# A hybrid decoder layer in split fp32r: from the pooling gates on, the tokens become the stationary operand and 512 weight columns the moving one

## The chip, the core and the metric

The kernel runs on one core of one Trainium2 chip, as one launch. The metric is the device time of that core in microseconds (us); before the change it is 2078.82 us, the median of three runs. The engines are named as in the profile: PE is TensorE's matmuls and PEld its loads of the stationary operand, ACT is ScalarE, DVE is VectorE, POOL is GpSimd, and SP is the sync engine, whose queue issues the weight transfers.

## The reference

One layer over 256 tokens of 2048 features, batch 1, all float32. Cut to what matters:

```
h      = rmsnorm(x, g_pre_mix)
proj   = h @ w_in                # -> z, xbc, dt, u_pool, gate_ssm, gate_pool
y_ssm  = mamba2_branch(...)      # 4096 features;   y_pool = pooling branch, 2048 features
merged = sigmoid(gate_ssm) * (y_ssm @ w_ssm_out) + sigmoid(gate_pool) * (y_pool @ w_pool_out)
x      = x + rmsnorm(merged @ w_mix_out, g_post_mix)
g, u   = split(rmsnorm(x, g_pre_ffn) @ w_ffn_in)          # 5632 features each
x      = x + rmsnorm((silu(g) * u) @ w_ffn_out, g_post_ffn)
x      = x + sigmoid(x @ w_ple_gate) * (p @ w_ple_proj)
```

## The kernel before

**Layout.** Everything between the first and the last transposition is features x tokens: a tile holds 128 features on the partitions and the 256 tokens in the free dimension. So a product takes a 128x128 block of weights as the stationary operand, streams the 256 tokens of one 128-feature block of the input through it, and leaves 128 output features x 256 tokens in PSUM.

**Precision.** A float32 operand is split in two fp32r parts, hi and lo, and a product is three matmuls: hi x hi, lo x hi and hi x lo. For the weights ACT makes the hi part (`w_hi`, a copy; `hi_units`), DVE the lo part (`w_lo`, a subtraction; `lo_units`). The same is done once for each operand built on the chip (`h_hi`/`h_lo`, `m_hi`/`m_lo`, `act_hi`/`act_lo`, `p_hi`/`p_lo`).

**The stream of weights.** All weights come in *units*: two 128-row blocks of 512 columns, 512 KB. `w_raw`, `w_hi` and `w_lo` are rings of four. SP issues unit u when DVE has finished unit u-4, ACT splits unit u when PE has used unit u-4, DVE follows ACT, PE follows DVE. A unit costs PE 2 blocks x 4 groups of 128 columns x 3 = 24 matmuls of 256 moving columns:

```
for n in columns:
    o = accum[:, n, :]
    wh = w_hi[:, s, a, P * n:P * n + P]
    wl = w_lo[:, s, a, P * n:P * n + P]
    mm(o, wh, hi[:, b, :], b == 0 and n % 2 == 0, False)
    mm(o, wh, lo[:, b, :], False, False)
    last = mm(o, wl, hi[:, b, :], False, b == blocks - 1)
```

**Order.** The stages run in a fixed order written out for each engine: the B/C projections, eight SSD groups, the pooling branch; then those that the change touches, 492 units in all: PO (pooling gate and `w_pool_out`, 64 units), SO (SSM gate and `w_ssm_out`, 96), MIX (`w_mix_out`, 32), FF (`w_ffn_in`, 11 chunks of 16 = 176), FO (`w_ffn_out`, 88), PP (`w_ple_proj`, 4), PG (`w_ple_gate`, 32). A product accumulates in `acc[0]` or `acc[1]` (two PSUM banks each), and ACT or DVE take it out while the next one runs (`acc_taken`). Work between units is hung in by `after=` hooks: what stands at hook k of an engine comes in its own order right after its unit k.

**Norms.** ACT squares the accumulated chunk, DVE adds three of the four chunks, and PE sums over the partitions with a float32 matmul against `mean_w`, which leaves the mean at every partition (`three_quarters`, `last_quarter`, `x1_squares`, four matmuls each). Then ACT takes the root, DVE the reciprocal of 256 columns, and `residual` multiplies and adds. The last chunk of MIX and of PG is done in two halves, so that what follows can begin on the first.

**Output.** `rows_out` turns 128x128 blocks of the result on PE, ACT or DVE copies them to `o_rows`, SP sends them out. The transposed x goes to DRAM at the start (`xT_scratch`) and comes back before FF (`x_back`).

## Time and profile before

| | |
|---|---|
| median of three runs | 2078.82 us (2078.63 to 2080.57) |
| span of the profiled execution, first to last instruction | 2083.3 us |
| mean granted TensorE clock in it | 0.994 |
| PE busy, PEld busy | 99%, 98% |
| DVE busy, ACT busy | 59%, 48% |
| moved by DMA | 384.55 MB, mean 185 GB/s |

Of the profiled execution only the span is known; it is 4.5 us above the median of the plain runs. Busy time of PE is a union over pipelined instructions (one matmul record lasts 0.28 us while the next starts some 0.12 us later), so the pace of the matmuls is read from counts over stretches, not from the duration of one.

### The profile page before, as it was taken

The numbers are of one execution on the slowest core, as the hardware profiler recorded it, in microseconds if no ns is written. First come the engines' busy times: TensorE is split into PE (matmuls) and PEld (weight loads), VectorE is DVE, ScalarE is ACT, GpSimd is POOL, SyncE is SP. The second block draws the span as 40 slices with busy tenths as digits, with TensorE's granted clock in tenths as the row PEclk, the third lists the DMA queues.
The fourth block names the chain that finished last, engine by engine and source line by source line (L and its number), as shares of the span: only waits on it lengthen the run. The fifth ranks groups of instructions, "written<-read, shape, count | busy, mean of one in ns | idle before, by whom it ended". The sixth has DMA issues, their size and how long they took to land.

```text
span 2083.3 us, 42373 instructions
## 1 busy us (share of the span) xinstructions
PE 2056.3 (99%) x17268; PEld 2042.0 (98%) x17268; DVE 1238.2 (59%) x1293; ACT 1002.5 (48%) x1149; POOL 2.4 (0%) x40
## 2 busy tenths in 40 slices
PE   7999999999999999999999989999999999999999
PEld 6999999999999999999999989999999999999998
DVE  5877888888776444444444475555555554444474
ACT  4545666666646444344444464444444443444453
POOL 0000000000000000000000000000000000000000
PEclk8999999999999999999999999999999999999999
DMA  6666666666565666555555646666666665555454
GB/s 207 203 203 192 188 190 191 186 186 188 171 191 189 186 182 183 188 184 183 184 187 183 218 131 184 187 184 182 184 187 182 183 188 185 183 186 187 158 189 140
DMA packets 199813, 384.55 MB, mean 185 GB/s; under 512 B 12176, under 2 KB 19504, under 8 KB 198448
## 3 DMA queue, kind: packets, MB, share of 16 engines
q1 hardware_dynamic: 199504, 381.16, 59.2%
q10 hardware_dynamic: 224, 2.16, 0.3%
q8 instruction: 65, 1.06, 0.2%
q14 instruction: 20, 0.16, 0.0%
HBM read 379.01 MB, written 4.26 MB: 184 GB/s over the span
## 4 chain that ended last, share of the span: by engine, by line
PE 98%; DVE 1%; ACT 1%; SPq 0%; issue 0%; DMA 0%; ACTq 0%
PE acc L397 94%; PE bank L397 2%; PE pair L397 1%; PE bank L400 0%; DMA dsk_row<-in_d_skip_dram 0%; PE pair L400 0%; ACT w_hi L661 0%; SPq L290 0%; ACT L661 0%; DVE csum L1258 0%; DVE w_lo L1037 0%; PE acc L400 0%; SPq L286 0%; DVE yrstd L1222 0%; DVE rstd L1048 0%
## 5 line engine op out<-in xcount | busy, mean ns | idle before, releaser
L1037 DVE TENSOR_TENSOR w_lo<-w_raw,w_hi 128x1024 fp32r<-128x1024 f32 (+1 forms) x696 | 847.7, 1221 | 801.9 <-ACT w_hi L661 801.8
L661 ACT ACTIVATE w_hi<-w_raw 128x1024 fp32r<-128x1024 f32 (+1 forms) x696 | 732.6, 1057 | 953.7 <-PE acc L397 946.7
L397 PE MATMUL acc<-h_hi,w_hi 128*128 128x256 f32 x3712 | 1052.6, 284 | 12.7 <-DVE h_lo L1044 6.3
L397 PE MATMUL acc<-h_lo,w_hi 128*128 128x256 f32 x3712 | 1044.4, 281 | 0.0
L397 PE MATMUL acc<-h_hi,w_lo 128*128 128x256 f32 x3712 | 1044.3, 281 | 0.0
L397 PEld LDWEIGHTS acc<-h_hi,w_hi 128*128 128x128 f32 x3712 | 702.4, 189 | 15.9 <-issue 8.2
L397 PEld LDWEIGHTS acc<-h_lo,w_hi 128*128 128x128 f32 x3712 | 702.4, 189 | 2.2 <-issue 1.9
L397 PEld LDWEIGHTS acc<-h_hi,w_lo 128*128 128x128 f32 x3712 | 702.2, 189 | 0.0
L397 PE MATMUL acc<-act_hi,w_hi 128*128 128x256 f32 x704 | 198.1, 281 | 0.0
L397 PE MATMUL acc<-act_lo,w_hi 128*128 128x256 f32 x704 | 197.9, 281 | 0.0
L397 PE MATMUL acc<-act_hi,w_lo 128*128 128x256 f32 x704 | 197.9, 281 | 0.0
L397 PE MATMUL acc<-y_lo,w_hi 128*128 128x256 f32 x512 | 144.0, 281 | 0.0
L397 PE MATMUL acc<-y_hi,w_lo 128*128 128x256 f32 x512 | 144.0, 281 | 0.0
L397 PE MATMUL acc<-y_hi,w_hi 128*128 128x256 f32 x512 | 143.9, 281 | 0.0
L397 PEld LDWEIGHTS acc<-act_hi,w_hi 128*128 128x128 f32 x704 | 132.9, 189 | 0.0
L397 PEld LDWEIGHTS acc<-act_lo,w_hi 128*128 128x128 f32 x704 | 132.9, 189 | 0.0
L397 PEld LDWEIGHTS acc<-act_hi,w_lo 128*128 128x128 f32 x704 | 132.9, 189 | 0.0
L397 PEld LDWEIGHTS acc<-y_hi,w_hi 128*128 128x128 f32 x512 | 96.7, 189 | 0.0
L397 PEld LDWEIGHTS acc<-y_lo,w_hi 128*128 128x128 f32 x512 | 96.7, 189 | 0.0
L397 PEld LDWEIGHTS acc<-y_hi,w_lo 128*128 128x128 f32 x512 | 96.7, 189 | 0.0
L397 PE MATMUL acc<-m_hi,w_hi 128*128 128x256 f32 x256 | 72.2, 282 | 0.0
L397 PE MATMUL acc<-m_hi,w_lo 128*128 128x256 f32 x256 | 72.0, 281 | 0.0
(186 smaller groups left out, 1613.9 us busy)
## 6 DMA issues: line engine op xcount, KB each, us to landing
w_raw<-in_w_in_dram SPq DMA_DIRECT2D x256, 512.0 KB, 3.8
w_raw<-in_w_ffn_in_dram SPq DMA_DIRECT2D x176, 512.0 KB, 3.7
w_raw<-in_w_ffn_out_dram SPq DMA_DIRECT2D x88, 512.0 KB, 3.6
w_raw<-in_w_ssm_out_dram SPq DMA_DIRECT2D x64, 512.0 KB, 3.6
w_raw<-in_w_pool_out_dram SPq DMA_DIRECT2D x32, 512.0 KB, 3.7
w_raw<-in_w_mix_out_dram SPq DMA_DIRECT2D x32, 512.0 KB, 3.6
w_raw<-in_w_ple_gate_dram SPq DMA_DIRECT2D x32, 512.0 KB, 3.6
decay<-cum_scratch SPq DMA_DIRECT2D x8, 1024.0 KB, 6.1
```

What stands on the lines that cost most here:

```text
L397: return nc.tensor.matmul(o, lhsT=l, rhs=r, start=first, stop=last, skip_group_check=True)
L661: return nc.scalar.activation(o, i, fn, **kw)
L1037: v.tensor_tensor(low, raw, high.bitcast(F32), ALU.subtract).then_inc(w_lo_done, 1)
```

## The change

From PO on, `row_product` takes the place of `product`. A 128-token block of the input is now stationary, and the 512 columns of a weight block stream past it; the result is 128 tokens x 512 features, one PSUM bank for each half of the tokens. A unit is 2 blocks x 2 halves x 3 = 12 matmuls of 512 moving columns. `acc_rows` are the same banks as `acc`.

The next product needs its input as features x tokens again, so the merged chunks (`turn_merged`), the FFN's activations (`turn_act`), the x after the mixers (`turn_x1`) and the x after the FFN (`turn_x2`) are turned on PE in 128x128 blocks, into `pair` or into four half-bank `pieces`. Norms are now along the free dimension: ACT squares with a running sum per token (`row_squares`), DVE adds four numbers, root and reciprocal are on one column. The gains of the post-norms come as rows broadcast to all partitions (`gain_mix`, `gain_ff`). x is read again as it lies in DRAM, so the trip of the transposed x is gone, and so are the matmuls against `mean_w` behind the first norm, `rows_out`, and the copies to `o_rows`: the output leaves as it is computed. The loads of x, the gain and p move from SP's queue to ACT's, at hook 3 of MIX's first chunk.

```diff
-            sp.wait_ge(unit_used, 4 * Q_MIX)
-            sp.wait_ge(xT_stored, 16)
-            sp.dma_start(x_back[:, :, :], xT_dram).then_inc(xT_landed, 16)
-            sp.dma_start(p_in[:, :, :], p_rows).then_inc(p_landed, 16)
...
+            for j in range(NQ - 1):
+                sp.wait_ge(o_ready, j + 1)
+                sp.dma_start(out_rows[:, :, CW * j:CW * j + CW], o_tok[:, j]).then_inc(out_stored, 16)
+            for a in range(2):
+                sp.wait_ge(o_ready, NQ + a)
+                sp.dma_start(out_rows[:, a, D - CW:D], o_tok[:, NQ - 1, a]).then_inc(out_stored, 16)
...
+            def row_products(q, k0, k, blocks, hi, lo, rows, halves):
+                s = (k0 + k) % RING
+                for i in range(2):
+                    b = 2 * k + i
+                    wh, wl = w_hi[:, s, i, :], w_lo[:, s, i, :]
+                    for a in halves:
+                        t = slice(P * a, P * a + P)
+                        mm(rows[:, a, :], hi[:, b, t], wh, b == 0, False)
+                        mm(rows[:, a, :], hi[:, b, t], wl, False, False)
+                        last = mm(rows[:, a, :], lo[:, b, t], wh, False, b == blocks - 1)
+                return last
+            def row_product(c, q, k0, blocks, hi, lo, rows, wait_for=None, after=None, halves=False):
+                pe.wait_ge(acc_taken, c - 1)
+                units = blocks // 2
+                for k in range(units):
+                    if wait_for:
+                        wait_for(k)
+                    if not halves or k < units - RING:
+                        pe.wait_ge(w_lo_done, 4 * q + k0 + k + 1)
+                    elif k == units - RING:
+                        for late in range(k, units):
+                            pe.wait_ge(w_lo_done, 4 * q + k0 + late + 1)
+                            last = row_products(q, k0, late, blocks, hi, lo, rows, (0,))
+                        last.then_inc(half_done, 1)
+                    own = (1,) if halves and k >= units - RING else (0, 1)
+                    row_products(q, k0, k, blocks, hi, lo, rows, own).then_inc(unit_used, 1)
+                    if after:
+                        after(k)
+            def turn_chunk(src):
+                for n in range(NB):
+                    for a in range(2):
+                        last = turn(pair[:, n, P * a:P * a + P], src[:, a, P * n:P * n + P])
+                return last
+            def turn_piece(halves, k, turned):
+                for n in range(2):
+                    for a in range(2):
+                        c = P * (2 * k + n)
+                        last = turn(pieces[k % 4][:, n, P * a:P * a + P], halves[a][:, c:c + P])
+                last.then_inc(turned, 1)
...
-                product(C_PO + 2 * j, Q_PO + 4 * j, 0, KB, h_hi, h_lo, acc[0])
-                product(C_PO + 1 + 2 * j, Q_PO + 4 * j, 8, KB, yp_hi, yp_lo, acc[1],
-                        wait_for=lambda k: k % 2 == 0 and yp_quarter(k))
+                row_product(C_PO + 2 * j, Q_PO + 4 * j, 0, KB, h_hi, h_lo, acc_rows[0])
+                row_product(C_PO + 1 + 2 * j, Q_PO + 4 * j, 8, KB, yp_hi, yp_lo, acc_rows[1],
+                            wait_for=lambda k: k % 2 == 0 and yp_quarter(k))
+            def turn_merged(j):
+                pe.wait_ge(fam["op_m"][0], j + 1)
+                if not (isinstance(j, int) and j == 0):
+                    pe.wait_ge(fam["op_m"][2], j)
+                turn_chunk(prod).then_inc(m_turned, 1)
+            def so(j, first):
+                row_product(C_SO + 2 * j, Q_SO + 6 * j, 0, KB, h_hi, h_lo, acc_rows[0],
+                            after=lambda k: k == 3 and not first and turn_merged(j - 1))
+                row_product(C_SO + 1 + 2 * j, Q_SO + 6 * j, 8, 2 * KB, y_hi, y_lo, acc_rows[1])
...
-                product(C_MIX + j, Q_MIX + 2 * j, 0, KB, m_hi, m_lo, acc[j % 2],
-                        wait_for=lambda k: j == 0 and k % 2 == 0 and pe.wait_ge(fam["op_m"][2], k // 2 + 1),
-                        after=lambda k: j == NQ - 1 and k == 5 and three_quarters(RMS_MIX, sqs1),
-                        halves=j == NQ - 1)
-            for half, ready, count in ((0, sq_half, 1), (1, sq_ready, NQ * RMS_MIX + NQ)):
-                pe.wait_ge(ready, count)
-                for n in (2 * half, 2 * half + 1):
-                    last = mm(ss, mean_w[:, :], sq1[:, (NQ - 1) % 2, n, :], False, n == NB - 1)
-            last.then_inc(sq_used, 1)
...
+                row_product(C_MIX + j, Q_MIX + 2 * j, 0, KB, m_hi, m_lo, acc_rows[j % 2],
+                            wait_for=lambda k: j == 0 and k % 2 == 0 and pe.wait_ge(fam["op_m"][2], k // 2 + 1),
+                            after=lambda k: j == 0 and k == 3 and turn_merged(NQ - 1), halves=j == NQ - 1)
+            def turn_x1(k):
+                pe.wait_ge(x1_ready, (2, 3, 4, 4, 5, 5, 6, 6)[k])
+                if k >= 4:
+                    pe.wait_ge(fam["op_h"][2], PIECES + k - 3)
+                turn_piece((x1[:, 1, :], x1[:, 0, :]), k, x1_turned)
...
+            row_product(C_FF, Q_FF, 0, KB, h_hi, h_lo, acc_rows[0], after=x1_ahead,
+                        wait_for=lambda k: pe.wait_ge(fam["op_h"][2], PIECES + k + 1))
...
+            def turn_act(j):
+                pe.wait_ge(acc_taken, C_FF + 2 * j + 2)
+                if isinstance(j, int) and j == 0:
+                    pe.wait_ge(fam["op_p"][2], 1)
+                else:
+                    pe.wait_ge(fam["op_ff"][2], j)
+                turn_chunk(uff).then_inc(ff_turned, 1)
...
+            def ff(j):
+                row_product(C_FF + 2 * j, Q_FF + 4 * j, 0, KB, h_hi, h_lo, acc_rows[0],
+                            after=lambda k: k == 4 and turn_act(j - 1))
+                row_product(C_FF + 1 + 2 * j, Q_FF + 4 * j, 8, KB, h_hi, h_lo, acc_rows[1])
...
+            def turn_x2(k):
+                pe.wait_ge(x2_ready, (2, 4, 6, 6, 8, 8, 10, 10)[k])
+                if k >= 4:
+                    pe.wait_ge(fam["op_x2"][2], k - 3)
+                turn_piece((fg[:, 0, :], fg[:, 1, :]), k, x2_turned)
...
-            def rows_out(j):
-                pe.wait_ge(o_ready, j + 1)
-                if not (isinstance(j, int) and j == 0):
-                    pe.wait_ge(rows_ready, j)
-                for a in range(2):
-                    for n in range(NB):
-                        last = turn(pair[:, 2 * a:2 * a + 2, :].rearrange("p b t -> p (b t)")[:, P * n:P * n + P],
-                                    o_T[:, n, P * a:P * a + P])
-                last.then_inc(ot_done, 1)
...
+                if c == NQ - 1:
+                    for k in range(4):
+                        turn_x2(k)
+                row_product(C_PP + c, Q_PP, c, 2, p_hi, p_lo, acc_rows[c % 2])
...
+                row_product(C_PG + j, Q_PG + 2 * j, 0, KB, h_hi, h_lo, acc_rows[j % 2],
+                            wait_for=lambda k: j == 0 and pe.wait_ge(fam["op_x2"][2], k + 1),
+                            after=lambda k: j == 0 and k + 4 < PIECES and turn_x2(k + 4), halves=j == NQ - 1)
...
+            def merged_hi(j):
+                act.wait_ge(m_turned, j + 1)
+                f(m_hi[:, ds(4 * j, 4), :], pair[:, :, :]).then_inc(fam["op_m"][1], 1)
...
+                        act.wait_ge(unit_used, 4 * Q_MIX)
+                        act.dma_start(x_rows_in[:, :, :], x_rows).then_inc(tok_landed, 16)
+                        act.dma_start(gain_mix[:, :], g_post_mix.to_broadcast([P, D])).then_inc(tok_landed, 16)
+                        act.dma_start(p_in[:, :, :], p_rows).then_inc(tok_landed, 16)
...
+            act.wait_ge(half_done, 1)
+            row_squares(RMS_MIX, NQ - 1, 0, acc_rows[1])
+            act.wait_ge(row_sum, 1)
+            row_root(RMS_MIX, slice(0, 1), 4 * EPS)
+            hi_units(Q_FF, 0, 2)
+            act.wait_ge(unit_used, 4 * Q_FF)
+            row_squares(RMS_MIX, NQ - 1, 1, acc_rows[1])
+            act.wait_ge(row_sum, 2)
+            row_root(RMS_MIX, slice(1, 2), 4 * EPS)
+            hi_units(Q_FF, 2, 2)
...
+                    last = f(h_hi[:, b, :], pieces[k % 4][:, n, :], scale=vecs[:, V_PRE_FFN + b:V_PRE_FFN + b + 1])
+                last.then_inc(fam["op_h"][1], 1)
...
+                if lag and k == 7:
+                    act.wait_ge(ff_turned, j)
+                    f(act_hi[:, ds(4 * (j - 1), 4), :], pair[:, :, :]).then_inc(fam["op_ff"][1], 1)
...
+            def post_gain(j, gain, rows):
+                cols = slice(CW * j, CW * j + CW)
+                by_feature = gain[:, cols].unsqueeze(1).to_broadcast([P, 2, CW])
+                v.tensor_tensor(fg[:, :, cols], rows, by_feature, ALU.mult).then_inc(acc_taken, 1)
...
+                v.scalar_tensor_tensor(x1[:, 1 - a, c0:c1], fg[:, a, c0:c1], rows_std[:, RMS_MIX, a:a + 1],
+                                       x_rows_in[:, a, c0:c1], ALU.mult, ALU.add).then_inc(x1_ready, 1)
...
+            last_gain(0)
+            row_inverse(RMS_MIX, 0)
+            dve.wait_ge(row_rstd, 1)
+            x1_part(0, 0, D)
+            lo_units(Q_FF, 0, 2)
+            dve.wait_ge(row_sq, 2 * NQ)
+            row_sums(RMS_MIX, 1)
+            last_gain(1).then_inc(acc_taken, 1)
+            row_inverse(RMS_MIX, 1)
+            dve.wait_ge(row_rstd, 2)
+            dve.wait_ge(acc_taken, C_FF)
+            x1_part(1, 0, 2 * P)
+            x1_part(1, 2 * P, 4 * P)
+            lo_units(Q_FF, 2, 1)
+            x1_part(1, 4 * P, 8 * P)
             for k in range(PIECES):
-                if k + 1 == PIECES - 2:
...
+                x1_low(k)
                 if k:
                     lo_units(Q_FF, k + 2, 1)
+                if k < 2:
+                    x1_part(1, (8 + 4 * k) * P, (12 + 4 * k) * P)
...
+                        dve.wait_ge(ff_turned, j - 1)
+                    for a in range(2):
+                        last = v.scalar_tensor_tensor(uff[:, a, :], acc_rows[1][:, a, :], rows_aux[:, 1, a:a + 1],
+                                                      graw[:, a, :], ALU.mult, ALU.mult)
+                    last.then_inc(acc_taken, 1)
...
+                    lo_part("op_ff", j, act_lo[:, four, :], pair[:, :, :], act_hi[:, four, :])
...
+                    v.scalar_tensor_tensor(fg[:, a, c0:c1], fg[:, a, c0:c1], rows_std[:, RMS_F, a:a + 1],
+                                           x1[:, 1 - a, c0:c1], ALU.mult, ALU.add).then_inc(x2_ready, 1)
...
+            dve.wait_ge(row_sq, 4 * NQ + 2)
+            v.tensor_reduce(rows_std[:, RMS_F, :], ssq[:, RMS_F, :, :], axis=AX.X, op=ALU.add).then_inc(row_sum, 1)
+            post_gain(NQ - 1, gain_ff, acc_rows[1])
+            dve.wait_ge(row_std, 4)
+            both = rows_std[:, RMS_F, :]
+            v.reciprocal(both, both).then_inc(row_rstd, 1)
+            dve.wait_ge(row_rstd, 6)
+            dve.wait_ge(acc_taken, C_PP)
+            x2_part(0, 2 * P)
+            x2_part(2 * P, 4 * P)
+            x2_part(4 * P, 8 * P)
+            lo_units(Q_PP, 3, 1)
...
+                lo_part("op_x2", k + 1, h_lo[:, 2 * k:2 * k + 2, :], pieces[k % 4], h_hi[:, 2 * k:2 * k + 2, :])
+                lo_units(Q_PG, k, 1)
+                if k < 2:
+                    x2_part((8 + 4 * k) * P, (12 + 4 * k) * P)
```

## Rows read from the trace of the kernel before

**Rows 1.** The page, part 1: busy us (share of the span) and instructions.

```profile
PE 2056.3 (99%) x17268; PEld 2042.0 (98%) x17268; DVE 1238.2 (59%) x1293; ACT 1002.5 (48%) x1149; POOL 2.4 (0%) x40
```

**Rows 2.** The page, part 4: the chain that ended last, by engine.

```profile
PE 98%; DVE 1%; ACT 1%; SPq 0%; issue 0%; DMA 0%; ACTq 0%
```

**Rows 3.** Groups by shape: busy us, mean ns of one, idle before and its releaser.

```profile
L1037 DVE TENSOR_TENSOR w_lo<-w_raw,w_hi 128x1024 fp32r<-128x1024 f32 x692 | 844.9, 1224 | 796.5 <-ACT w_hi L661 796.3
...
L661 ACT ACTIVATE w_hi<-w_raw 128x1024 fp32r<-128x1024 f32 x692 | 730.1, 1059 | 948.0 <-PE acc L397 941.0 <-DMA w_raw<-in_w_in_dram 6.0 <-PE bank L397 0.5
...
L397 PEld LDWEIGHTS acc<-h_hi,w_hi 128*128 128x128 f32 x3712 | 702.4, 189 | 15.9 <-issue 8.2 <-DVE h_lo L1044 6.7 <-DVE w_lo L1037 0.6
```

**Rows 4.** The chain in order of time, whole span: start us, us, what.

```profile
577.93 615.45 PE acc L397 x5184
1193.38 1.73 PE bank L397 x8
...
1216.38 1.73 PE bank L397 x8
...
1237.97 692.06 PE acc L397 x5832
1930.03 1.73 PE bank L397 x8
```

**Rows 5.** Four stretches: us, each engine busy (instructions), granted clock, DMA share, GB/s.

```profile
680.00:1180.00 500.00, 500.00 (x4216) 500.00 (x4215) 234.08 (x193) 210.69 (x210) 0.00 (x0) 1.00 0.58 185
1250.00:1900.00 650.00, 650.00 (x5480) 650.00 (x5479) 341.45 (x284) 266.85 (x260) 0.00 (x0) 1.00 0.61 184
1206.50:1209.50 3.00, 3.00 (x15) 3.00 (x15) 3.00 (x4) 2.46 (x5) 0.00 (x0) 0.50 0.00 0
1197.79:1205.95 8.16, 1.98 (x11) 1.28 (x9) 6.38 (x8) 6.27 (x11) 0.00 (x0) 0.81 0.43 127
```

**Rows 6.** The same chain from 1925 us on, five pieces of it.

```profile
1968.82 1.03 ACT sq_f L661
...
1969.90 2.00 PE bank L397 x8
...
2065.05 0.87 PE pair L400 x8
...
2079.33 0.67 PE pair L400 x4
...
2080.03 0.69 DVE o_rows L1443
```

**Rows 7.** Groups by shape, DVE.

```profile
L1186 DVE TENSOR_TENSOR decay<-decay,cbm 128x2048 f32<-128x2048 f32 x8 | 18.3, 2284 | 0.0
...
L1225 DVE SCALAR_TENSOR_TENSOR yg<-yg,vecs,yrstd 128x256 f32<-128x256 f32 x32 | 13.4, 480 | 1.0
...
L1438 DVE SCALAR_TENSOR_TENSOR o_T<-tgate,ple 128x512 f32<-128x512 f32 x2 | 1.4, 692 | 9.0 <-ACT tgate L661 9.0
...
L1180 DVE TENSOR_TENSOR to_end<-decay,tok_cum 128x8 f32<-128x8 f32 x8 | 1.3, 158 | 0.0
```

**Rows 8.** Groups by shape, ACT: busy us, mean ns of one, idle before.

```profile
L661 ACT ACT_TABLE_LOAD x25 | 32.1, 1283 | 1.2 <-PEq L1458 0.8
...
L661 ACT ACTIVATE sq<-acc 128x512 f32<-128x512 f32 x2 | 1.2, 598 | 4.9 <-PE acc L397 4.9
```

**Rows 9.** DMA from 1175 to 1215 us: rate by slice; issues with KB, us to landing.

```profile
GB/s 336 39 219 272 287 303 410 410 442 315 369 401 399 393 395 297 68 16 0 0 63 219 289 201 254 119 313 104 10 0 0 0 0 0 0 113 375 53 0 104
...
w_raw<-in_w_ffn_in_dram SPq DMA_DIRECT2D x9, 512.0 KB, 5.0
x_back<-xT_scratch SPq DMA_DIRECT2D x1, 2048.0 KB, 9.6
```

More of the change, by code:

```diff
@@ L649, in _ @@
-            for half in range(2):
-                pe.wait_ge(o_ready, NQ + half)
-                pe.wait_ge(rows_ready, NQ - 1)
-                for a in range(2):
-                    for n in range(2):
-                        last = turn(pair[:, 2 * half + a, P * n:P * n + P], o_T[:, 2 * half + n, P * a:P * a + P])
-                last.then_inc(ot_done, 1)
+                    row_product(C_FO + j, Q_FO + t * (FO_UNITS // 2), FO_UNITS * i, FF // P, act_hi, act_lo,
+                                acc_rows[i],
+                                wait_for=lambda k: j == 0 and k % 2 == 0 and pe.wait_ge(fam["op_ff"][2], k // 2 + 1),
+                                after=lambda k: j == 0 and k == 4 and turn_act(NFF - 1))
@@ L879, in _, with post_squares @@
                 so(j, Q_SO + 6 * j, False)
-            def post_take(stage, j, q, k_end, accum, first, squares, gain, between=None):
+            def post_squares(stage, j, q, k_end, rows):
                 summed(q, k_end)
-                if j == NQ - 1:
-                    act.wait_ge(sq_added, SQ_ADDED[stage] + 1)
-                f(squares[:, j % 2] if j else first, accum[:, :, :], ACT.Square).then_inc(sq_ready, 1)
-                if between:
-                    between()
-                for n in range(NB):
-                    col = gain + NB * j + n
-                    last = f(fg[:, NB * j + n, :], accum[:, n, :], scale=vecs[:, col:col + 1])
-                last.then_inc(acc_taken, 1)
+                for a in range(2):
+                    row_squares(stage, j, a, rows)
             for j in range(NQ):
```

420 lines of the change are left out of this document (184 added, 236 removed).

## The prediction, made blind

> **What bounds the kernel now.** The page's first part comes first: PE and its weight loads are busy through 99% and 98% of the span, DVE 59%, ACT 48% [rows 1]. A union of pipelined records says only that PE is hardly ever without work, so the chain that ended last is next: 98% of it is PE [rows 2]. The groups by shape confirm it from the other side: nearly all idle time of ACT before its weight splits ends with PE, and DVE's ends with ACT [rows 3]. Nothing waits long for a transfer. So what counts is how many nanoseconds PE needs from one matmul to the next, and the counts give that: 615.45 us for 5184 and 692.06 us for 5832 matmuls in a row, 118.7 ns each [rows 4], which agrees with 500 us for 4216 and 650 us for 5480 [rows 5].
>
> Where do the 118.7 ns go? In 1206.5:1209.5 the granted clock is at its lower level, 1.2 GHz, and 15 records touch 3.00 us, 14 spacings of 214 ns: 256 columns at one per cycle are 213.3 ns, so next to nothing comes on top [rows 5]. At 2.4 GHz, the clock of the long stretches, 256 columns are 106.7 ns, so here 12.0 ns are on top of each. The float32 matmuls against `mean_w` are the third point: eight records of 256 columns in 1.73 us, 216.3 ns each at full clock [rows 4]; eight turns of 128 columns take 0.87 us, 109 ns each [rows 6]. The 128 further columns cost 107.5 ns, two cycles each, so such a record streams for 213.3 ns with 3.0 ns on top, although each has a fresh 128x128 stationary block too. The surcharge is thus about 12 ns where streaming lasts 107 ns in fp32r and 0 to 3 ns where it lasts 213 ns. I read it as a load of the next block that just fails to hide behind 107 ns of streaming. The change doubles the streaming per load.
>
> **The products.** From PO on there are 492 units of two blocks, 984 blocks. Before, a block is 4 x 3 = 12 matmuls, 11,808 in all: x 118.7 ns = 1401.6 us. After, it is 2 x 3 = 6 of 512 columns, 5,904 in all. Columns in total stay the same. The trace has no fp32r matmul of 512 columns, so I bound it. From below: 512 columns at 2.4 GHz with nothing on top, 213.3 ns, 1259.3 us. From above: the whole surcharge stays, 213.3 + 12.0 = 225.3 ns, 1330.2 us; further above, the cost goes with the columns, 2 x 118.7 = 237.4 ns, and nothing is gained. The nearest row is the `mean_w` record, which streams just as long: 216.3 ns [rows 4], 1277.0 us. I take that: **-124.6 us**.
>
> The Trainium skill (TensorE: Matmul & The Clock Gate, "Back-to-back issue gap") gives N/2.4 + 2.5 ns between warm matmuls. For 512 columns that is an estimated 215.8 ns, near the row; for 256 columns it is 109.2 ns, where this trace has 118.7. By the rule alone a split into two costs 2.5 ns, 15 us over all, and the change would have no more to win; but the kernel before is timed by its trace, and behind the change the rule ends at the forecast's own time.
>
> **The turns.** Added while PE streams: merged 4 x 8, activations 11 x 8, x1 4 pieces x 4 (the first four pieces fall into a gap, below), x2 8 x 4: 168 turns x 109 ns [rows 6] = **+18.3 us**; p is turned before and after. Removed: three `rows_out` of eight, **-2.6 us**. None should make PE wait. `turn_act` stands after PE's unit 4, some 13 us into a chunk of 2.6 us units; its input is ready after a split of ACT (1.06), of DVE (1.22, [rows 3]) and two operations of 0.69 us on 512 columns [rows 7], under 5 us. Behind it on ACT are the copy out of `pair` and the split of unit 8, on DVE the lo part and its own: some 5 us after unit 4, while PE reaches unit 8 after 8.7. For `turn_merged`, after unit 3, DVE has its two operations behind its unit 4, ready by about 8 us of 10.4. If this cover were gone, each of the 15 groups would cost its wait whole.
>
> **The norms.** In the stream of before stand the three quarters of MIX, four groups for x1, the three quarters of F: 6 x 1.73 = 10.4 us [rows 4]; at the end of FO PE waits 1.1 us for a square (1.03), then sums for 2.0 [rows 6]. All of it goes: **-13.5 us**.
>
> **MIX to FF.** Before, PE's last product of MIX ends at 1197.79 and the first of FF starts at 1205.95, 8.16 us, with a few sums between [rows 5]. After, the first half of the tokens is ready 4 x 6 x 0.216 = 5.2 us before the end. ACT squares it (0.60, [rows 8]), loads a table (1.28) and takes the root; DVE goes on with gain (0.69), a residual of 2048 columns (2.28), two splits (2.44) and is free 2.5 us after the end. Then, in its queue: sum 0.16, gain 0.69, reciprocal 0.16, two parts 0.96, a split 1.22, a part 0.69, two lo operations 0.96 [rows 3, 7], 4.8 in all, 5.0 with hand-overs: PE starts at 7.5 us, **-0.6 us**. DVE sets it, no longer PE's sums and a reciprocal of 256 columns. The clock is at its lower level after this gap before [rows 5]; I expect it after too, at the same price.
>
> **FO to PG.** The second PP product waits for the gain of the last chunk, 0.5 us more than the first product covers, and the first four pieces of x2 are turned only before the last PP product, so that their splits come just in time or 0.3 us late. Adding DVE's and ACT's queues with the same rows gives 1.7 us of idle PE in four places: **+1.7 us**; with no overlap it might be 4, and 0 at best.
>
> **The end and the transfers.** The last four turns (0.67) and the copy (0.69) leave the chain [rows 6]: **-1.4 us**. 512 KB in 2.6 us are 202 GB/s against 185 now; the slices reach 442 [rows 9]. x, the gain and p, 3.4 MB, are issued by ACT behind its unit 3 and needed by DVE some 24 us later; 2 MB landed in 9.6 us beside the stream, and the units' own in 5.0 [rows 9]; the second gain, 1 MB, has all of FO's first chunk. SP's queue loses two issues. All this is hidden; were the 3.4 MB late, DVE would stand before PE did by up to 5 us. The start loses a store nobody waits for: nothing.
>
> **Sum.** -124.6 + 18.3 - 2.6 - 13.5 - 0.6 + 1.7 - 1.4 = **-122.7 us**. On the traced span, 2083.3 to 1960.6; the plain runs are 4.5 us under the span, so on their median 2078.8 - 122.7 = **1956 us**.
>
> **The rivals.**
> *The surcharge stays.* If the 12 ns belong to each exchange of the stationary block, or loading disturbs the fp32r stream for a fixed time, 225.3 ns: -71.4 + 1.9 = -69.5, **2009 us**. For it: the nearest row is float32, a column in two cycles, and fp32r streams one in each. Against: nothing on top at the lower clock, where the load is as long.
> *No cheaper per column.* 237.4 ns: **2081 us**, no change. For it: only that no 512-column fp32r row exists. Against: the surcharge of 12 ns at one clock and about 0 at the other.
> *Hand-overs late.* A wait of 2 us at each of 15 turn groups and 5 more at the two boundaries: **1991 us**. Against: the 4 us of slack counted above.
> *Slower.* The load of the token block is not hidden behind the longer stream: one load record lasts 189 ns [rows 3], so a matmul would take up to 402 ns, 2376 us for the products, **about 3055 us**. It decides from 24 ns exposed on (237.4 - 213.3). The Trainium skill (the same page, "The mechanism") says that a load overlaps a running matmul only where the row groups differ, and all here use the full array. The trace disagrees: 118.7 ns is less than 106.7 of streaming and 189 of loading one after the other [rows 3, 4].
>
> **How the numbers follow.** Forecast 1956 with 0.63, surcharge stays 0.19, late hand-overs 0.09, no cheaper 0.04, slower 0.05. The forecast's own range is 1938 (213.3 ns) to 1972. The range reaches to the surcharge case, 1938 to 2012, and leaves out about 0.1. Within 0.2%, 4 us, is what a measurement of this kernel can't tell from no change. Faster 0.91, same 0.04, slower 0.05.
>
> **What would show it.** In the profile after: 5,904 matmuls of 512 columns, some 216 ns apart, about 12 in 2.6 us; 184 turns more and 32 fewer, 109 ns each, with no idle PE before `turn_act`; DVE 1.22 and ACT 1.06 us a unit as before, and ACT still waiting for PE; a gap of 7 to 8 us before FF; 202 GB/s in FF. A pace of 225 ns would be the first rival. Wrong altogether would be PE idle time that ends with DVE or ACT in every chunk, or load records without a matmul over them.

## The result, and the profile after

The change makes the kernel 1.0% faster: 2058.86 us (2058.14 to 2059.14, four runs) against 2078.73 (2077.59 to 2080.57), a ratio of 0.9897 with a 95% interval of 0.9881 to 0.9913. The forecast was 1956 us with a range of 1938 to 2012. The sign held and the size did not: 20 us came where 123 were forecast.

The page of the changed kernel, part 1, answers to [rows 1]:

```profile
PE 2034.5 (99%) x11452; PEld 1750.5 (85%) x11452; DVE 1206.6 (59%) x1284; ACT 984.6 (48%) x1139; POOL 2.4 (0%) x40
```

PE has 5,816 records fewer and is still busy through 99% of the span. The weight loads fell from 98% to 85%, so they are hidden as the prediction said, and the time did not follow. The chain in order of time (start, length, what) is to be read against [rows 4]:

```profile
905.43 0.87 PE pair L401 x8
906.30 67.22 PE acc L398 x288
...
1257.87 0.87 PE pair L401 x8
1258.74 44.81 PE acc L398 x192
...
1715.49 240.95 PE acc L398 x1032
```

There are whole chunks without any other engine on the chain, and 240.95 us for 1,032 products are 233.5 ns each (233.3 from start to start). The windows say the same over both long stretches of [rows 5]:

```profile
680.00:1180.00 500.00, 500.00 (x2162) 402.66 (x2161) 239.28 (x197) 208.78 (x208) 0.00 (x0) 1.00 0.61 193
1250.00:1900.00 650.00, 650.00 (x2834) 524.27 (x2833) 321.02 (x273) 267.29 (x272) 0.00 (x0) 1.00 0.59 186
```

Full clock, no idle time, and 193 and 186 GB/s instead of 185 and 184. The timeline of PE (start, length) shows how regular it is; the starts are 0.23 us apart, and in the trace's nanoseconds the spacings repeat 231, 232, 237: exactly 700 ns for three products and 2,800 for a unit of twelve.

```profile
800.27 0.40 PE L398 MATMUL acc<-w_hi,h_hi 128*128 128x512 f32 x1
800.50 0.39 PE L398 MATMUL acc<-w_lo,h_hi 128*128 128x512 f32 x1
800.74 0.39 PE L398 MATMUL acc<-w_hi,h_lo 128*128 128x512 f32 x1
800.97 0.40 PE L398 MATMUL acc<-w_hi,h_hi 128*128 128x512 f32 x1
```

So the products are the question. From PO on there are 492 units: 2.848 us each before (24 x 118.67 ns), 2.800 after. That is 1401.2 and 1377.6 us of the spans. What is left behind the start of PO is 2083.3 - 649.1 - 1401.2 = 32.9 us before and 2057.4 - 647.5 - 1377.6 = 32.3 after (649.1 and 647.5 are the starts of the last product ahead of PO). The spans differ by 25.9 us: 23.6 from the pace, 0.7 from all else together, 1.6 from the time ahead of PO, which the prediction had put at nothing. The medians differ by 19.9, since the span of the traced execution of before is 4.5 us above its median and that of after 1.5 below. The plain runs of before spread by 3 us, so the two small parts aren't told from noise.

Part of the 1.6 us has a cause in the two traces. Up to PO both kernels have the same products at the same places, and both run them at 117.3 to 117.4 ns at 560 us. In the trace of before the pace becomes 118.7 ns behind an idle time of 0.2 us at 577.9 us and stays so to the end; that of after has the same idle time and stays at 117.3 up to PO. The same stretch, before and then after:

```profile
605.00:645.00 40.00, 40.00 (x340) 40.00 (x339) 29.98 (x35) 22.32 (x27) 0.00 (x0) 1.00 0.54 170
605.00:645.00 40.00, 40.00 (x343) 40.00 (x343) 30.25 (x36) 22.60 (x30) 0.00 (x0) 1.00 0.57 172
```

So the 118.7 ns, from which the prediction and the 23.6 us start, is one of two paces that this code has shown. At 117.3 ns throughout, the 11,808 products of before would take an estimated 16 us less, and the change would win about 8 us on the products.

### The profile page after: what moved, and what is told of

Same layout as the page of the kernel before. It is cut to its first block, busy times and chain, and to the rows that moved or that the text cites. A ratio compares the mean times of both kernels' runs of the same rounds, so it can differ in the third digit from the quotient of the medians.

```text
span 2057.4 us, 30692 instructions
## 1 busy us (share of the span) xinstructions
PE 2034.5 (99%) x11452; PEld 1750.5 (85%) x11452; DVE 1206.6 (59%) x1284; ACT 984.6 (48%) x1139; POOL 2.4 (0%) x40
## 4 chain that ended last, share of the span: by engine, by line
PE 97%; DVE 1%; ACT 0%; SPq 0%; DMA 0%; issue 0%; ACTq 0%
PE acc L398 94%; PE bank L398 1%; PE pair L398 1%; PE pair L401 1%; PE bank L401 1%; DVE w_lo L1086 0%; DMA dsk_row<-in_d_skip_dram 0%; DVE x L1408 0%; ACT w_hi L726 0%; SPq L295 0%; DVE csum L1309 0%; ACT L726 0%; PE acc L401 0%; SPq L291 0%; DVE yrstd L1273 0%
## 5 line engine op out<-in xcount | busy, mean ns | idle before, releaser
L398 PE MATMUL acc<-h_hi,w_hi 128*128 128x256 f32 x1536 | 437.9, 285 | 6.8 <-DVE h_lo L1093 6.6
L398 PE MATMUL acc<-w_hi,h_lo 128*128 128x512 f32 x1088 | 431.4, 397 | 0.0
L398 PE MATMUL acc<-w_hi,h_hi 128*128 128x512 f32 x1088 | 431.0, 396 | 0.2 <-DVE w_lo L1086 0.2
L398 PE MATMUL acc<-h_lo,w_hi 128*128 128x256 f32 x1536 | 430.7, 280 | 0.0
L398 PE MATMUL acc<-h_hi,w_lo 128*128 128x256 f32 x1536 | 430.6, 280 | 0.0
L398 PE MATMUL acc<-w_lo,h_hi 128*128 128x512 f32 x1088 | 430.0, 395 | 0.0
L398 PEld LDWEIGHTS acc<-h_hi,w_hi 128*128 128x128 f32 x1536 | 289.8, 189 | 9.6 <-DVE h_lo L1093 7.0
L398 PEld LDWEIGHTS acc<-h_lo,w_hi 128*128 128x128 f32 x1536 | 289.9, 189 | 2.1 <-issue 1.9
L398 PEld LDWEIGHTS acc<-h_hi,w_lo 128*128 128x128 f32 x1536 | 289.7, 189 | 0.0
L398 PEld LDWEIGHTS acc<-w_lo,h_hi 128*128 128x128 f32 x1088 | 204.6, 188 | 49.8
```

Source lines behind the costliest of these rows:

```text
L398: return nc.tensor.matmul(o, lhsT=l, rhs=r, start=first, stop=last, skip_group_check=True)
```

## The experiments

Seven small kernels issue matmuls: m1 and m3 to m7 with nothing beside them that matters, m2 with a ring of weights streaming. Their paces are read from the records' start times over the last 24 spacings of each stretch. A count in a window takes in the one or two instructions that were running when it opened.

### What 512 float32r columns cost by themselves, and in halves

```
for i in range(96):                                      # m1: one such loop for each kind; shortened
    mm(b[..][:, 0:512], at(tok, i), cols(wgt, i, 512), ...)
```
```diff
-                        mm(rows[:, a, :], hi[:, b, t], wh, b == 0, False)
-                        mm(rows[:, a, :], hi[:, b, t], wl, False, False)
-                        last = mm(rows[:, a, :], lo[:, b, t], wh, False, b == blocks - 1)
+                        for c in (0, 256):
+                            o, n = rows[:, a, c:c + 256], slice(c, c + 256)
+                            mm(o, hi[:, b, t], wh[:, n], b == 0 and c == 0, False)
+                            mm(o, hi[:, b, t], wl[:, n], False, False)
+                            last = mm(o, lo[:, b, t], wh[:, n], False, b == blocks - 1)
```

m1_pace: 

> A kernel of TensorE products alone: x is read, made into float32r and bf16 tiles, and each line then issues 96 or 192 matmuls of one kind back to back; nothing else runs, and the output is a copy of x, not the layer's. Four theories of why the 512-column product takes 233.3 ns apart where 216.3 was forecast. Per column: a float32r product costs about 0.455 ns for every column whatever its length, so 512, 384, 256 and 128 columns are 233, 175, 117 and 58 to 60 ns apart, also with one stationary tile for all, with 64 tokens and with four banks in turn. Load: what is above 213.3 is the stationary load beside it, so one stationary tile for all or a 64-column one takes 512 columns to about 216, and 128 columns are limited by their load. Type: bf16 columns cost less than float32r ones, so 512 bf16 columns are 213 to 217 ns apart and 512 float32r ones 233. Data: the pace depends on what is multiplied, so zeros as the moving operand run at 213 to 217.

m2_pace_busy: 

> The same products, with a ring of weights streaming beside them: 512 KB transfers, ACT copies of 1,024 columns and VectorE subtractions of 1,024 columns, as the layer has them. The output is a copy of x. Per column, load, type and data: each line as in the quiet kernel, within 1%. Contention: the quiet kernel has 512 float32r columns at 213 to 217 ns and only here they are at 233, because the moving operand is read beside the writes of the ring.

e1_split: 

> The changed kernel with every 512-column product cut into two of 256 columns: tokens stay stationary and weights move as in the change, but the number of products is again 11,808. Per column: the two halves cost 2 x 117.3 to 118.7 ns, so the time is 2,060 to 2,068 us, within 0.5% of the changed kernel, and all that the change gained lies outside the products. Load or a fixed cost for each product: the number of products matters, so the time goes back up by 5,904 times the fixed part, 30 us or more above the changed kernel (2,089 or more). Contention of the moving weights: with 256 columns moving they are dearer than the 117.3 of the stationary weights, above 120 ns.

Windows of m1 over equal stretches of 512 columns float32r, the same with one stationary tile, 512 bf16, 256 float32r, 256 bf16; then m2's first:

```profile
31.00:51.00 20.00, 20.00 (x90) 16.55 (x90) 0.00 (x0) 0.00 (x0) 1.00 0.00 0
114.00:134.00 20.00, 20.00 (x89) 16.53 (x89) 0.00 (x0) 0.00 (x0) 1.00 0.00 1
202.00:222.00 20.00, 20.00 (x95) 9.09 (x93) 0.00 (x0) 0.00 (x0) 1.00 0.00 1
70.00:90.00 20.00, 20.00 (x169) 20.00 (x168) 0.00 (x0) 0.00 (x0) 1.00 0.01 2
223.00:243.00 20.00, 20.00 (x186) 17.92 (x184) 0.00 (x0) 0.00 (x0) 1.00 0.00 1
```
```profile
32.00:52.00 20.00, 20.00 (x90) 16.55 (x90) 13.56 (x12) 11.80 (x12) 0.00 (x0) 1.00 0.88 301
```

| ns from start to start | 512 | 384 | 256 | 128 |
|---|---|---|---|---|
| float32r | 226.7 | 173.3 | 120.0 | 111.7 |
| bf16 | 215.8 | | 109.2 | |
| float32 | | | 215.8 for each of two records | |

One stationary tile for all, half of its rows, four banks in turn and zeros as the moving operand: 226.7 each; 64 stationary columns: 230.0. With 301 GB/s, ACT and DVE beside it, still 226.7. So data and contention fall, and so does the load theory as it was put: neither one stationary tile for all nor 64 columns of it brought 216. But no line was without a load; the window from 114 us, with one tile for all, has 89 loads for 89 products, 186 ns each. The loads of the whole kernel by type, float32r, bf16 and float32:

```profile
L97 PEld LDWEIGHTS b<-wgt,tok 128*128 128x128 f32 x1157 | 169.7, 192 | 32.7 <-ACT nul_r L80 17.6
L97 PEld LDWEIGHTS b<-wgt_b,tok_b 128*128 128x128 bf16 x288 | 28.1, 98 | 13.8 <-issue 0.4
L97 PEld LDWEIGHTS b<-x_in 128*128 128x128 f32 x64 | 12.2, 190 | 1.7
```

The type matters: bf16 and float32 have 2.5 ns on top of their streaming and float32r 13.3. The duration of the load doesn't explain that, since float32's is as long as float32r's; that a load disturbs the float32r stream is not excluded. Here the surcharge is the same 13.3 ns at 512, 384 and 256 columns, a fixed part of each product. The Trainium skill (TensorE: Matmul & The Clock Gate, "Back-to-back issue gap") has N/2.4 + 2.5 ns for what it calls the isolated gap of warm matmuls; bf16 agrees with 215.8 and 109.2, float32r does not. But 226.7 is not the layer's 233.3, and the plain law per column missed too (384 and 256 columns cost more than their share).

e1 took 2098.33 us (ratio 1.0095, 1.0078 to 1.0112), above all of the per-column range: 120.0 ns for each half. Its chain over the stretch that took 240.95 us:

```profile
1746.69 247.74 PE acc L398 x2064
```

By the bounds set beforehand that speaks for a fixed part of each product. The next runs showed that this reading was too simple.

### Order or place

```
layer: (h_hi, w_hi) (h_hi, w_lo) (h_lo, w_hi), two halves of the tokens, two banks   # the layer's addresses
far:   (h_hi, far)                                                                  # another moving tile
```

m3_order: 

> TensorE alone again, 512 columns of float32r unless said, with the tiles where the layer has them and in its order: in turn the layer's unit of products (high tokens by high weights, high by low, low by high, in two banks), the same in one bank, with the two low products exchanged, one product repeated, pairs in which only the moving or only the stationary tile changes, one tile pair throughout, the quiet kernel's order with and without a changing moving window, halves of 256 columns, 384 columns, the unit behind eight turns, low tokens first, 64 tokens, and the old kernel's order (weights stationary, 256 token columns moving). The output is a copy of x. The quiet kernel had 226.7 ns for each 512 columns where the layer has 233.3. Order theory: the sequence of tiles makes the difference, so the layer's unit takes 233.3 here too and one of the simpler orders 226.7. Surroundings theory: the order is innocent and the 6.7 ns come from what runs beside the products in the layer (semaphore waits, the ring's writes), so every 512-column line here takes 226.7. Address theory: only the layer's addresses matter, so all lines with its tiles take 233.3 and those with the far tile 226.7. The old order takes 117.3 to 120 in all three.

Every one of the ten 512-column lines with 128 tokens and the ring's tiles took 233.3 ns: any order, one bank, even one pair of tiles repeated. The two with `far` as the moving tile took 226.7. Halves took 120.0, 64 tokens 231.3, the old order 118.7. That is the address theory: the ring begins at 159.84375 KB behind a base of 16,512 bytes, at byte 180,192, and the tokens at 16,512.

### The place of the two tiles

```diff
-    RING0 = 159.84375
+    RING0 = 159.8125      # e2 and b1: after and before, ring 32 bytes lower
+    RING0 = 159.75        # e3 and b2: 96 bytes lower
```
```
run(512, left, 0, far, offset)     # m4 and m5: one pair of tiles, the offsets varied
```

m4_place: 

> TensorE alone, one stationary and one moving tile of float32r again and again, with the place of each in the memory shifted in steps: first the moving tile of 512 columns at byte offsets 0, 4, 8, 16, 32, 48, 64, 96, 128, 256, 512, 864, 1024, 2048 and 4096 from a border of 4 KB, then the stationary one at 4, 32, 64, 96 and 512, then a moving tile near the top of the memory at 0 and 32, then 256 columns at 0, 32, 64 and 96 and with the stationary tile at 32 and 64, and 384 columns at 0, 32 and 64. The output is a copy of x. In the runs so far tiles of the weight ring, which begins 32 bytes off a border of 64, took 233.3 ns for 512 columns and tiles on such a border 226.7. Alignment theory: 226.7 for offsets 0, 64, 128, 256, 512 and above, and 233.3 for those that are off a 64-byte border; the stationary tile's place does nothing. Region theory: near the top of the memory it is 233.3 whatever the offset, and offsets elsewhere do nothing. For 256 columns the alignment theory gives 120.0 at every offset, since both the aligned and the shifted ones showed that.

e2_ring64: 

> The changed kernel with the weight ring laid 32 bytes lower, so that every moving tile begins on a border of 64 bytes; nothing else differs. Alignment theory: 5,904 products at 226.7 instead of 233.3 ns, 39 us less than the changed kernel: 2,016 to 2,024 us. Region or surroundings theory: no change, 2,056 to 2,062 us.

b1_ring64: 

> The kernel before with the ring laid 32 bytes lower; there the ring's tiles are stationary and the moving tokens already lie on borders of 64 bytes. Alignment theory: no change, 2,075 to 2,083 us. If the stationary tile's place matters too, the products go from 118.7 to 117.3 ns and the time drops by about 16 us to 2,062, or they rise to 120.0 and it grows by as much.

m4, 512 columns: 226.7 with both tiles on the border, 236.7 with the moving one 4 bytes off, 233.3 at 32 and 96 and also at 128, 228.9 at 64, 226.7 at 256, 512, 1024 and above; 864, which is 96 beyond a multiple of 256, has 233.3. Moving the stationary tile by 32 or 64 bytes gives 233.3 as well, by 512 bytes 226.7. Windows at moving offsets 0, 32, 128 and 256:

```profile
31.00:41.00 10.00, 10.00 (x45) 8.26 (x44) 0.00 (x0) 0.00 (x0) 1.00 0.01 2
76.00:86.00 10.00, 10.00 (x44) 8.02 (x44) 0.00 (x0) 0.00 (x0) 1.00 0.00 0
109.00:119.00 10.00, 10.00 (x44) 8.05 (x43) 0.00 (x0) 0.00 (x0) 1.00 0.00 0
131.00:141.00 10.00, 10.00 (x46) 8.26 (x45) 0.00 (x0) 0.00 (x0) 1.00 0.00 0
```

So it is not a matter of a 64-byte border. In the layer the effect was large. e2: 2025.41 us (ratio 0.9757, 0.9738 to 0.9776), just above the 2,016 to 2,024 expected; its four runs range from 2021.8 to 2032.3, and the traced one is the fastest. b1, the old kernel with one number changed: 2018.13 us (0.9713, 0.9696 to 0.9729), where I had expected no change or 16 us either way; it beats the change. Chain of e2, then of b1 beside the 615.45 and 692.06 us of [rows 4]:

```profile
1684.34 236.44 PE acc L398 x1032
```
```profile
569.91 587.85 PE acc L397 x5184
...
1202.47 660.97 PE acc L397 x5832
```

e2's products take 228.9 ns, not the 226.7 expected; b1's take 113.3.

m5_grid: 

> TensorE alone, one stationary and one moving tile of float32r, each at byte offsets 0, 32, 64, 128, 192, 256 and 384 from a border of 4 KB: all 49 pairs with 512 columns (40 products each), then all 49 with 256 (48 products). The output is a copy of x. Seen so far at 512: 226.7 ns with both at 0, and 233.3 when either is moved by 32, 228.9 with the moving tile at 64, 226.7 again at 256. Relative theory: only the distance of the two tiles within 256 bytes counts, so the pace is the same along every diagonal of the table. Absolute theory: each tile has good and bad places of its own, so rows and columns of the table are good or bad whatever the other tile does. Floor: no pair is under 226.7 for 512 columns or under 113.3 for 256, so at its best place a column costs the same in both lengths, 0.443 ns.

e3_ring128: 

> The changed kernel with the weight ring 96 bytes lower than it was, where ring and tokens lie alike within 256 bytes. Relative theory: 226.7 ns for each of the 5,904 products instead of 228.9 with the ring 32 bytes lower, so 13 us less than that kernel, 2,007 to 2,014 us. Absolute theory: a moving tile at 128 bytes took 233.3 in the quiet kernel, so back to 2,055 to 2,062 us.

b2_ring128: 

> The kernel before with the ring 96 bytes lower than it was. Relative theory: ring and tokens alike, which in the quiet kernel gave 120.0 ns for 256 columns, so 1.3 ns more than before for 11,808 products and as much for the earlier ones: 2,090 to 2,105 us. If its best pace needs only a 64-byte border, 113.3 ns and 2,014 to 2,022 us, as with the ring 32 bytes lower.

e4_split64: 

> The changed kernel with the ring 32 bytes lower and every 512-column product cut into two of 256. If a column costs the same in both lengths once the places are good, the time is that of the uncut kernel at the same ring, 2,017 to 2,030 us. If each product has a fixed part beyond its columns, 5,904 more products cost 20 us or more: over 2,040.

The grid, ns, stationary offset down, moving across:

```
512       0     32     64    128    192    256    384
  0    226.7  233.3  228.9  232.3  233.3  226.7  233.3
 32    233.3  226.7  233.3  233.3  234.2  233.3  233.3
 64    233.3  233.3  226.7  228.9  232.1  233.3  228.9
128    233.3  234.2  233.3  226.7  228.9  232.1  226.7
192    228.9  233.3  233.3  233.3  226.7  228.9  233.3
256    226.7  233.3  228.9  232.3  233.3  226.7  233.3
384    233.3  234.3  233.3  226.7  228.9  232.1  226.7

256: 120.0 on the whole diagonal; 113.3 at (0, 192), (64, 256), (128, 64), (256, 192), (384, 64);
     117.4 to 120.0 at all others
```

For 512 columns the relative theory holds: with the distance counted from the stationary to the moving tile within 256 bytes, every pair at distance 0 takes 226.7, every pair at 64 takes 228.9, every pair at 192 takes 233.3, and those at 128 take 232.1 to 233.3. From PO on the kernels' products lie like this: the changed kernel and e1 at distance 96, e2 and e4 at 64, e3 at 0; before at 160, b1 at 192, b2 at 0. For 256 columns distance 0 is the worst, and the five pairs at 113.3 all have distance 192, though three more at 192 have 117.8. Nothing is under 226.7 or under 113.3, and 2 x 113.3 is 226.7: at its best place a column costs 0.443 ns in both lengths, though the best places are not the same.

e3 took 2032.84 us (0.9776, 0.9757 to 0.9796), more than expected, and yet its products have the forecast pace:

```profile
1697.95 234.24 PE acc L398 x1032
```

The expectation had left out the first part of the kernel, where the ring is stationary: the last product ahead of PO starts at 658.9 us with this ring, at 637.2 with e2's. b2 has 120.0 ns early and late and took 2110.18 (1.0147, 1.0127 to 1.0168), above the 2,090 to 2,105 expected. e4 took 2061.75 (0.9898, 0.9866 to 0.993; single runs 2051.7 to 2063.5, the traced one the slowest), 117.8 ns for each half:

```profile
1716.81 243.22 PE acc L398 x2064
```

That is over the bound set for a fixed part, but the grid has 117.8 for 256 columns at this distance, 113.3 at others: what halving costs depends on the place too.

### The layer's own places, other types, and both places at once

```diff
-    RING0 = 159.84375
+    RING0 = 159.6875
+    w_hi_row = place("w_hi_row", ..., RING0 + 16.0625)     # e5: 128 within 256 bytes, from PO on
+    w_hi = place("w_hi", ..., RING0 + 16.125)              # 192 within 256 bytes, up to the pooling products
...
+            dve.wait_ge(unit_used, 4 * Q_PO)
```

m6_fine: 

> TensorE alone, one stationary and one moving tile. First 512 float32r columns with the moving tile at every 16 bytes from 16 to 496 and the stationary one at 0; then at the places that tokens (stationary, 128) and ring have within 512 bytes in the changed kernel (480) and with its ring 32 and 96 bytes lower (448, 384); then 256 columns with ring (stationary) and tokens (128) as in the kernel before (480) and with its ring 32 and 96 bytes lower; then six pairs of places in bf16 with 512 and with 256 columns; 128 float32r columns at 0, 32, 64 and 96; float32 at 0 and 96. The output is a copy of x. Relative theory: 233.3, 228.9 and 226.7 ns at the three places of the changed kernel and 118.7, 113.3 and 120.0 at those of the kernel before, as the layer showed, and 226.7 among the steps of 16 only at 256. Region theory: the layer's numbers come from something else of its surroundings, so these six lines differ from it by 1 ns or more. Type: bf16 takes 215.8 and 109.2 at every pair, if the places matter only for tiles of 4-byte values; if they matter for all, bf16 spreads by 2% or more too.

e5_two_places: 

> The changed kernel with two places for the ring's tiles: up to the pooling products, where they are stationary, 32 bytes below where they were, and from the pooling gates on, where they move, 96 below; VectorE waits once for the last pooling product before the places change. Relative theory: the early part as with the ring 32 bytes lower (its first gate unit ends at 637 us in the trace, against 659 at 96) and the late part as with 96 (1,372 us from there), and 1 to 2 us for the wait: a span of 2,009 to 2,013 us and a time of 2,009 to 2,016, the lowest of all. If the places aren't what sets the pace of either part, it falls between the two kernels with one place, 2,025 to 2,033 us.

In steps of 16 bytes 512 columns repeat exactly with a period of 256: 226.7 at 240, 256 and 496, otherwise 228.9 to 234.6. bf16 took 215.8 and 109.2 at all six pairs, float32 215.8 at both, 128 float32r columns 111.7 at all four. The three places of the changed kernel came out as in the layer to a tenth: 233.3, 228.9, 226.7. Those of the old one only in part: 117.3, 117.8 and 120.0 where the layer had 118.7, 113.3 and 120.0.

e5 took 2012.95 us (2010.51 to 2016.84; ratio 0.9668, 0.9648 to 0.9687), within its range: the last product ahead of PO starts at 636.6 (what its expectation calls the end of the first gate unit), and the late products have their best pace.

```profile
1678.05 234.27 PE acc L400 x1032
```

m7_history: 

> TensorE alone, float32r tiles at three pairs of places: 256 columns with stationary tiles at 448 and moving ones at 128 bytes (the kernel before with its ring 32 bytes lower), 256 with 480 and 128 (the kernel before), 512 with 128 and 480 (the changed kernel). For each pair eight stretches of 48 (36 for 512 columns) products: plain, after eight turns, after a pause in which TensorE waits for one ACT copy, after five products of 128 columns, after five of bf16, then in the layer's order with changing tiles, that after eight turns, and after a pause. The output is a copy of x. In the layer the first pair ran at 117.8 ns early and at 113.3 later, and the second at 117.3 and then 118.7. History theory: what comes just before a stretch decides between two paces at one place, so stretches of the first pair split into 113.3 and 117.8, those of the second into 117.3 and 118.7. Order theory: the plain stretches all have 117.8 and 117.3, and only those in the layer's order have the layer's 113.3 and 118.7. The third pair takes 233.3 in every stretch by the place theory; a stretch of 226.7 there would mean that history can undo a bad place.

Windows of m7: the first pair of places after turns, after a pause, in the layer's order, the same after turns; then the second pair plain, after turns, after a pause:

```profile
38.00:43.00 5.00, 5.00 (x45) 5.00 (x44) 0.00 (x0) 0.00 (x0) 1.00 0.00 0
45.00:50.00 5.00, 5.00 (x47) 5.00 (x46) 0.00 (x0) 0.00 (x0) 1.00 0.01 3
62.20:67.20 5.00, 5.00 (x46) 5.00 (x46) 0.00 (x0) 0.00 (x0) 1.00 0.01 3
69.00:74.00 5.00, 5.00 (x44) 5.00 (x44) 0.00 (x0) 0.00 (x0) 1.00 0.00 0
81.00:86.00 5.00, 5.00 (x44) 5.00 (x44) 0.00 (x0) 0.00 (x0) 1.00 0.00 0
88.00:93.00 5.00, 5.00 (x45) 5.00 (x45) 0.00 (x0) 0.00 (x0) 1.00 0.00 0
95.00:100.00 5.00, 5.00 (x44) 5.00 (x43) 0.00 (x0) 0.00 (x0) 1.00 0.02 3
```

The first pair runs at 117.8 or 113.3 ns, the second at 117.3, 118.7 or 120.0, each for as long as nothing interrupts. For the first pair every group of turns was followed by 117.8 and every pause by 113.3; the second changed behind turns, pauses and short runs of other products without such a rule. So history decides among a few paces that the place allows, and the layer's values at these two pairs of places are among them. The grids of 256 columns have one stretch for each pair, so their single values hold for their history too: stationary 64 and moving 0 took 113.3 in m4 and 117.8 in m5. In b1 itself both appear: 117.8 early and 113.3 later, the same tiles' places throughout:

```profile
60.00:80.00 20.00, 20.00 (x172) 20.00 (x171) 19.79 (x35) 11.55 (x12) 0.00 (x0) 1.00 0.58 173
700.00:900.00 200.00, 200.00 (x1768) 200.00 (x1767) 96.69 (x80) 86.40 (x83) 0.00 (x0) 1.00 0.62 193
```

The third pair, the changed kernel's, took 233.3 in all eight stretches. No history that was tried rescues it; only its place does. The spread of the plain runs fits this without showing it: the four kernels with 256-column products at distance 192 range over 3.7 to 11.7 us (b1, e5, e2, e4), the two that are at distance 0 throughout, e3 and b2, over 1.4 and 1.5.

## Why the prediction was wrong

**The failed step is the pace of the 512-column product.** "The nearest row is the `mean_w` record ... 216.3 ns": the products measured 233.3, so the term was not -124.6 but 5,904 x 233.3 - 11,808 x 118.7 = -24 us. The difference, 5,904 x 17.0 ns = 100 us, is nearly all of the 103 us by which the forecast missed.

**The reasoning behind it fell.** I read the 12 ns over 106.7 as a load that just fails to hide behind a short stream. m1 shows the same pace with one stationary tile for all and with half its rows. In float32r the surcharge is there at 512 columns too, where 213 ns of streaming outlast a load record of 188 to 192 ns, and at 256 columns it goes from 6.7 to 13.3 ns by place with the same load. bf16 has no such surcharge at 256 columns, but its load records are half as long (98 ns), so alone it would not settle this. The `mean_w` record was the wrong neighbour: float32 has no surcharge at any place tried, and float32r, 4 bytes for each column in one cycle, has one of 13.3 to 23.4 ns on 512 columns that goes by the distance of the two tiles within 256 bytes. That 4-byte columns at this rate compete with the load for reads of the memory would fit the three types and [rows 5], where nothing is on top at 1.2 GHz; it is argued, not shown.

**The rivals.** "No cheaper per column" (0.04) comes nearest in its time and, with each length at its best place, is exact: 226.7 is twice 113.3. At the layer's places it was 233.3 against 2 x 118.7, a gain of 4.0 ns for each pair by accident of place and, on the side of before, of history. That accident is 23.6 us of the 25.9 between the two traces; that the sign came out as forecast was in the main luck. "The surcharge stays" (225.3) is within 1.4 ns where the two tiles lie alike within 256 bytes, with 13.3 ns at three lengths (m1); at the layer's places its size was wrong, 12 ns before and 20 after. The range ended with this rival. Had the type of the nearest row been taken seriously, the upper bound of 237.4 would have deserved far more than 0.04.

**The terms that held.** All else was forecast as +1.9 us and measured as -0.7 between the two traces.

- Turns: 0.87 us for each group of eight, as in the chain above, with no idle PE ahead of them; units with a group are 873 to 896 ns longer.
- MIX to FF: PE's last product begins at 1188.61 and the first of FF at 1195.63, 7.0 us against 8.3 between the same records before; forecast 7.5 against 8.16. DVE ends it, as forecast. The waits and the timeline:

```profile
PE acc L398 <- DVE h_lo L1093: 6.6, 1, 6.6
```
```profile
1188.61 0.39 PE L398 MATMUL acc<-w_hi,m_lo 128*128 128x512 f32 x1
1191.82 1.97 PE L401 MATMUL bank<-ident,x 128*128 128x128 f32 x8 [2.81 <-DVE x L1408]
1194.01 1.97 PE L401 MATMUL pair<-ident,x 128*128 128x128 f32 x8 [0.23 <-DVE x L1408]
1195.63 0.78 PE L398 MATMUL acc<-w_hi,h_hi 128*128 128x512 f32 x1
```

- FO to PG: PP and PG take 104.9 us, of which 36 units of 2.8 and eight pieces of 0.44 are 104.3; 0.6 us more where 1.7 were forecast.
- Norms: the sums of 1.73 us [rows 4] are gone from the chain, and MIX is 0.9 us over 32 units of 2.8, one group of turns, where it was 1.7 over.
- The end: 5.0 us from the start of PE's last product instead of 6.4, -1.3 for -1.4. The last two pieces of work in the chain:

```profile
2053.41 0.70 DVE o_tok L1529
2054.14 0.69 DVE o_tok L1532
```

- Transfers: no wait of PE ends with one behind the start.

**Both designs at their best place.** From the last product ahead of PO to the end e3 takes 1371.9 us and b1 1375.8. Of this difference almost nothing is left for the change itself: b1's products fall back to 117.8 ns around 1180, from 1865 to 1902 and from 1949 us on, which costs 4.2 us over 113.3, while e3's are 0.8 us above 226.7 in all. Two of these stretches, where 30 us at 113.3 ns would hold 265 products:

```profile
1870.00:1900.00 30.00, 30.00 (x257) 30.00 (x257) 12.66 (x11) 11.41 (x11) 0.00 (x0) 1.00 0.53 177
1950.00:1980.00 30.00, 30.00 (x258) 30.00 (x257) 14.51 (x13) 13.07 (x13) 0.00 (x0) 1.00 0.56 189
```

So with the best pace on both sides, norms and end against turns come to about half a microsecond, as they did between before and after (0.7). The fastest kernel is e5, 2012.95 us; b1, one number in the old kernel, has 2018.13. Their ranges of single runs touch (2010.5 to 2016.8, 2015.5 to 2019.2), and their spans are 2010.9 and 2013.8.

## What to carry to other kernels

When one kind of instruction fills the span, take its price only from a row of the same data type, or measure it alone first; a row with the same streaming time in another type misled here by 17 ns in 216. In float32r, try the place of the two operands before the shape of the product: 32 bytes on the weight ring were worth 60 us of 2078 in the kernel before, three times what the change brought. A product's pace that is exact over hundreds of instructions and yet differs between stretches points to places and history, not to the traffic beside it.

## What the runs showed of the hardware

- Float32r products at full clock: 512 columns 226.7 to 236.7 ns, 256 columns 113.3 to 120.0, with the byte distance of stationary and moving tile, with a period of 256 bytes where it was stepped (512 columns). bf16 (215.8, 109.2) and float32 (215.8) did not vary at the places tried.
- 128 float32r columns take 111.7 ns, hardly less than 256 at their best (113.3).
- 256 columns have two or three paces at one pair of places, and a turn group, a wait or a few products of another kind can switch between them (117.8 and 113.3; 117.3, 118.7 and 120.0). The kernel before ran at 117.3 ns and then at 118.7 in one trace.
- At the lower level of the clock 512 float32r columns took 427 ns, 512 cycles of 1.2 GHz: no surcharge, as with 256 in [rows 5].
- A load record of a full 128x128 tile lasts 188 to 192 ns in float32r and float32 and 98 in bf16, and next to nothing of it shows in the pace of bf16 (109.2 ns for 256 columns) and float32 (215.8).
- Not settled: why the distance matters, what part the load of the stationary tile has in it, and what in a pause picks the pace.
